# x transposed unscaled and kept for the residual, and part of the output projection between attention steps

## The chip, the core and the metric

The kernel runs on one core of a Trainium2 chip. The metric is the device time of one execution in microseconds (us). A core has five engines that run side by side and meet at semaphores: TensorE (matrix products and transposes, into eight banks of accumulators), VectorE, ScalarE (ACT), GpSimd (POOL) and SyncE (SP), which here issues nearly all loads and stores to 16 DMA engines.

## What is computed

One layer of a hybrid encoder over 320 rows: 256 prompt frames and 64 sample frames, 1024 features, all in 32-bit floats. Cut to what matters here:

```python
h = rms_norm(x, p['norm_mix'])            # x * rsqrt(mean(x^2) + eps) * gain
proj = h @ p['w_in']                      # u, z, a, b, cq, ckv, kpe
...                                       # o_gdn: 4 recurrent (gated delta) heads
...                                       # o_mla: 4 latent-attention heads
mix = jnp.concatenate([o_gdn.reshape(B, S, GDN_VW), o_mla.reshape(B, S, MLA_HEADS * V_DIM)], axis=-1)
x = x + mix @ p['w_out']
h = rms_norm(x, p['norm_mem'])            # then attention over 256 memory tokens
x = x + om.reshape(B, S, MEM_HEADS * MEM_HEAD_DIM) @ p['w_mo']
h = rms_norm(x, p['norm_ffn'])            # then a router and 32 experts, top 4
x = x + y.reshape(B, S, D)
```

Each expert has three weight matrices of 1024 x 1024, so 12.6 MB, and all 32 are run.

## The kernel before

The kernel is written engine by engine, in one order per engine; `CHAIN` lists the steps of the first part in the order in which every engine takes its share of them. Nothing is scheduled by a tool: the order of the code is the order of each queue, and semaphores (`wait_ge`, `then_inc`) join the queues. `mark` and `at` set and read one-time events of an engine.

**Layouts.** Rows are kept in three blocks of 128, 128 and 64 (`TB` = 3, `b`); features in eight blocks of 128 (`KD` = 8, `k`). `x3` is x by rows. `hT` is feature-major: `hT[:, k, :]` is feature block k on the partitions and 320 columns. A product of a 128 x 128 weight block with `hT[:, k, :]` is one `mm` of 320 columns; in the trace it is two MATMUL instructions, since the operands are 32-bit. A transpose (`tr`) is one.

**Start.** SP loads x, the constants (`CO`: identity, ones, masks, the epsilon column) and then the blocks of `w_in`. ACT issues ten small loads (the convolution's rows and eight gain vectors) and squares the three row blocks (`squares`). VectorE and POOL turn the sums into reciprocal norms (`rstd`, `root`), VectorE scales the rows into `xs3`. TensorE transposes the convolution's rows and the gains, then the scaled rows in `norm_transposes`, 24 transposes over banks 0 and 1 in turn; ACT copies each bank into `hT` with the gain `c_mix` (`feature_major`). Then `project(pos, ...)` works through `RING`: each position is a tile of 128 outputs, eight products over k, banks 0 and 1 in turn, moved out by ACT in `evacuate`.

**Middle.** Recurrent heads and latent attention are prepared in `CHAIN`. The recurrent heads' results (`o_gdn`) stand in `hT[:, 0:4, :]` before the attention starts; the attention heads' results go to `hT[:, 4:8, :]` one by one. `attention("mla", ...)` has 12 units (3 row blocks x 4 heads) and 15 steps n; in a step TensorE does the scores of unit n, transposes the probabilities of unit n-2 and multiplies those of unit n-3 with the values. Between the steps `conv_states_and_x(n)` is called on TensorE and ACT: from n = `XT_AT` = 7 on it transposes one feature block k of x, which SP has loaded a second time into `x3`, over banks 6 and 7, and ACT copies it to `xT[:, k, :]` and scales a block of the memory queries' weights (`wmq_sb`) with the gain.

**Output projection.** For each k, eight products of `wout_sb` with `hT` (i = 0 to 3 the recurrent heads, 4 to 7 the attention heads) in bank k % 2; `x2_add(k)` on VectorE adds them to `xT[:, k, :]`, and four products of the memory queries follow for the block before. Then comes the memory attention (`attention("mem", ...)`), the router, and the experts.

**Experts.** Weights stream through nine slots of 2 MB (`slot_sb`, `tile_at`; six tiles an expert). Slots 0 to 5 are the tile `weights`, 6 lies in `stream`, 7 in `small_weights`, 8 is `more_weights` (`W2`), which nothing else uses. `first_tiles` fills a slot for the first time, as the space comes free; `refill` waits for `tile_used`, that is for TensorE to have gone through the tile nine places before.

## Time and profile before

| | us |
|---|---|
| Median of 3 runs | 1323.24 (1319.42 to 1323.3) |
| The profiled execution | 1321.59, span 1319.8 |
| TensorE busy in the span | 1275.2 (97%) |
| VectorE, ACT, GpSimd busy | 462.7, 215.1, 19.5 |
| Loaded and stored | 440.53 MB, mean 334 GB/s |

The profile is one execution. Its page lists busy time and the chain of work that ended last: followed back from the last instruction, at each step to what released it. Four stretches can be told apart: the first part up to the attention (to 248 us), the attention with its last steps (to 283), the output projection and memory attention (to 384), and, after the router, the experts from 401 on. TensorE's granted clock is 1.00 (2.4 GHz) or 0.50 (1.2 GHz). A busy TensorE is not one at its peak: ends of matmuls are modelled, and a few records can be missing.

### The profile page before, as it was taken

To read this page: it belongs to the slowest core of one execution; us is meant where nothing else is said; L and a number is where in the kernel's file an instruction comes from. 1 tells how busy PE (TensorE), PEld (TensorE's weight loads), DVE (VectorE), ACT (ScalarE), POOL (GpSimd) and SP (SyncE) were. 2 spreads that over 40 slices of the span, in tenths; PEclk is the share of its full clock that TensorE was granted. 3 is DMA by queue.
4 is the path that set the end of the run, shared out by engine and by line. 5 is a ranking of instruction groups with operands and counts; after the bars stand their busy time and mean duration, and the time that the engine had idled before them with its cause. 6 is when DMAs were issued, how large, how long until landed. Compare 5 with 4: busy or idle time off the path is not lost.

```text
span 1319.8 us, 21031 instructions
## 1 busy us (share of the span) xinstructions
PE 1275.2 (97%) x8602; PEld 580.3 (44%) x8602; DVE 462.7 (35%) x984; ACT 215.1 (16%) x573; POOL 19.5 (1%) x28
## 2 busy tenths in 40 slices
PE   5999999999999999999999999999999999999997
PEld 4677655567564333433333433333433333333332
DVE  2455234533664233322333322333322333322223
ACT  3551333740341000000000000000000000000000
POOL 0000011100000000000000000000000000000000
PEclk9999999989989999999999999999999999999999
DMA  9512100852238999999999999999999999999996
GB/s 337 216 65 89 42 29 16 296 200 110 80 124 344 428 428 427 429 429 429 429 428 429 429 428 428 428 428 429 429 429 429 429 429 429 429 428 429 429 428 261
DMA packets 48046, 440.53 MB, mean 334 GB/s; under 512 B 7635, under 2 KB 10169, under 8 KB 23334
## 3 DMA queue, kind: packets, MB, share of 16 engines
q1 hardware_dynamic: 47916, 439.90, 80.1%
q8 instruction: 29, 0.48, 0.1%
q14 instruction: 11, 0.09, 0.0%
q10 hardware_dynamic: 90, 0.06, 0.0%
HBM read 436.62 MB, written 3.33 MB: 333 GB/s over the span
## 4 chain that ended last, share of the span: by engine, by line
PE 78%; DMA 16%; DVE 3%; ACT 2%; issue 1%; POOL 1%; DVEq 0%; SPq 0%; POOLq 0%
PE bank L1053 74%; DMA weights<-in_w_gu 15%; PE bank L1056 3%; ACT scaled L614 1%; POOL stats L586 1%; DMA x<-in_x_sample 1%; ACT stream L614 0%; PE bank L1692 0%; DVE weights L1818 0%; DVE x L2391 0%; ACT weights L614 0%; DVE x L2240 0%; DVE stats L2161 0%; ACT small_weights L614 0%; DVE scaled L1822 0%
## 5 line engine op out<-in xcount | busy, mean ns | idle before, releaser
L2391 DVE SCALAR_TENSOR_TENSOR x<-bank,small_weights,x 128x512 f32<-128x512 f32 (+1 forms) x192 | 134.9, 744 | 598.5 <-PE bank L1053 598.5
L1053 PE MATMUL bank<-weights,small_weights 128*64 128x512 f32 (+4 forms) x1456 | 336.0, 588 | 3.1 <-DMA weights<-in_w_gu 3.1
L1053 PEld LDWEIGHTS bank<-weights,small_weights 128*64 128x64 f32 (+1 forms) x1456 | 105.7, 139 | 195.6 <-issue 171.6
L1053 PE MATMUL bank<-weights,scaled 128*64 128x512 f32 x704 | 155.9, 595 | 5.1 <-ACT scaled L614 5.1
L614 ACT ACTIVATE scaled<-bank 128x256 f32<-128x256 f32 (+5 forms) x153 | 58.2, 408 | 324.9 <-PE bank L1053 241.9
L614 ACT ACTIVATE scaled<-scaled 128x512 f32<-128x512 f32 x32 | 20.2, 631 | 550.0 <-DVE scaled L1822 550.0
L1053 PE MATMUL bank<-scaled,small_weights 64*128 64x512 f32 x384 | 108.1, 640 | 1.4 <-DVE x L2391 0.7
L1053 PE MATMUL bank<-stream,small_weights 128*64 128x512 f32 (+4 forms) x408 | 89.5, 547 | 2.1 <-DMA stream<-in_w_gu 1.1
L1053 PEld LDWEIGHTS bank<-weights,scaled 128*64 128x64 f32 x704 | 48.7, 137 | 97.1 <-issue 87.9
L1053 PE MATMUL bank<-small_weights 96*64 96x512 bf16 (+2 forms) x408 | 86.7, 497 | 0.5 <-DVE small_weights L1818 0.5
L1053 PEld LDWEIGHTS bank<-stream 128*128 128x128 bf16 (+1 forms) x2416 | 75.0, 100 | 27.5 <-issue 26.4
L1053 PE MATMUL bank<-small_weights,weights 128*128 128x320 f32 (+3 forms) x320 | 86.2, 419 | 0.6 <-ACT small_weights L614 0.6
L1053 PE MATMUL bank<-stream 128*128 128x64 bf16 (+1 forms) x2416 | 79.2, 196 | 1.1 <-ACT stream L614 1.1
L1053 PEld LDWEIGHTS bank<-small_weights,weights 128*128 128x128 f32 (+2 forms) x320 | 57.0, 190 | 24.8 <-issue 3.7
L1053 PE MATMUL bank<-weights 64*64 64x64 f32 (+5 forms) x752 | 65.7, 266 | 0.0
L1053 PEld LDWEIGHTS bank<-scaled,small_weights 64*128 64x128 f32 x384 | 29.0, 184 | 79.0 <-issue 75.9
L1053 PEld LDWEIGHTS bank<-small_weights 96*64 96x64 bf16 (+2 forms) x408 | 28.7, 128 | 70.0 <-issue 67.9
L1053 PE MATMUL bank<-small_weights,stream 128*128 128x320 f32 (+4 forms) x212 | 57.0, 427 | 0.0
L1053 PEld LDWEIGHTS bank<-stream,small_weights 128*64 128x64 f32 (+1 forms) x408 | 31.6, 146 | 51.3 <-issue 44.4
L1053 PEld LDWEIGHTS bank<-weights 64*64 64x64 f32 (+3 forms) x752 | 38.7, 144 | 22.4 <-issue 21.0
L1053 PEld LDWEIGHTS bank<-small_weights,stream 128*128 128x128 f32 (+1 forms) x212 | 37.4, 195 | 16.8 <-issue 3.5
L1053 PE MATMUL bank<-more_weights,small_weights 128*64 128x512 f32 x176 | 40.2, 598 | 0.5 <-DMA more_weights<-in_w_gu 0.5
(194 smaller groups left out, 903.1 us busy)
## 6 DMA issues: line engine op xcount, KB each, us to landing
weights<-in_w_gu SPq DMA_DIRECT2D x85, 2048.0 KB, 26.9
weights<-in_w_down SPq DMA_DIRECT2D x44, 2048.0 KB, 28.3
stream<-in_w_gu SPq DMA_DIRECT2D x21, 2048.0 KB, 28.1
more_weights<-in_w_gu SPq DMA_DIRECT2D x11, 2048.0 KB, 27.7
small_weights<-in_w_gu SPq DMA_DIRECT2D x11, 2048.0 KB, 26.2
small_weights<-in_w_down SPq DMA_DIRECT2D x10, 2048.0 KB, 28.2
more_weights<-in_w_down SPq DMA_DIRECT2D x10, 2048.0 KB, 28.4
weights<-in_w_in SPq DMA_DIRECT2D x4, 2048.0 KB, 14.4
```

Source lines behind the costliest of these rows:

```text
L586: pool.tensor_tensor(tile, tile, minus_half[0:tile.shape[0], :].broadcast_to(list(tile.shape)), ALU.pow).then_inc(sem("root_ready"), 1)
L614: return act.activation(out, in_, func, **kw)
L1053: return pe.matmul(out, lhsT, rhs, start=start, stop=stop)
L1056: return pe.transpose(out, in_, ident[0:in_.shape[0], 0:in_.shape[0]])
L2391: dve.scalar_tensor_tensor(xx, PS[bank][0:rows, :], gcur[0:rows, b:b + 1], xx, ALU.mult, ALU.add)\
```

## The change

Five things change.

1. **Start.** x is loaded as three blocks with semaphores of their own. The first 260 columns of the constants, put in another order, come by ACT's queue, ahead of the small loads; the rest by SP behind the first block of `w_in`, which is split in two. TensorE transposes the unscaled x3, block by block as it arrives, into all eight banks; ACT copies each bank to `xraw`, which lies in `W2`. ACT squares two row blocks and VectorE the third; ACT takes the reciprocal root with a logarithm and an exponential. VectorE writes the reciprocals on diagonals, TensorE multiplies these with ones, so that every partition has the row of 320 reciprocals, VectorE copies it to `rstd_rows`, and one operation per k makes `hT` from `xraw`, gain and `rstd_rows`. The first projection's product k waits for that `hT` block alone.
2. **No second load of x,** and no transposes of it between attention steps: `x2_add` reads `xraw`.
3. **Output projection.** Between the last attention steps TensorE does the products i = 0 to 3 of k = 0 and k = 1, into banks 6 and 7. After the attention only i = 4 to 7 remain for these two.
4. **Slot 8** is loaded for the first time behind the last `x2_add`, since `xraw` lies in it.
5. The loads of `w_out`'s two halves have semaphores of their own, and the loads of `b_gu` no longer wait for the transposes of x.

The diff, cut to its core:

```diff
-            load(x3[:, 0:2, :], b_major(x_prompt[0]), "ld_x")
-            load(x3[0:DEC, 2, :], x_sample[0], "ld_x")
-            load(CO[:, :], consts, "ld_const")
-            load(wqk_sb[:, :, 512:1024], k_major(w_in[0][:, 512:1024], 0, KD), "ld_win0")
+            for b in range(2):
+                load(x3[:, b, :], x_prompt[0][b * P:(b + 1) * P, :], f"ld_x{b}")
+            load(x3[0:DEC, 2, :], x_sample[0], "ld_x2")
+            for n in range(2):
+                load(wqk_sb[:, 4 * n:4 * n + 4, 512:1024], k_major(w_in[0][:, 512:1024], 4 * n, 4 * n + 4), f"ld_win0{'ab'[n]}")
+            load(CO[:, C_HEAD:C_N], consts[:, C_HEAD:C_N], "ld_const")
...
-            first_tiles(SLOTN - 1, SLOTN)
...
-            load(x3[:, 0:2, :], b_major(x_prompt[0]), "ld_x")
-            load(x3[0:DEC, 2, :], x_sample[0], "ld_x")
...
-            sp.wait_ge(sem("xT_tr"), KD)
...
+            sp.wait_ge(sem("x2_add"), KD)
+            first_tiles(SLOTN - 1, SLOTN)
             sp.wait_ge(*at("qm_mm"))
             first_tiles(0, 1)
...
+            act.dma_start(CO[:, 0:C_HEAD], consts[:, 0:C_HEAD]).then_inc(sem("ld_head"), 16)
...
+            for b in range(2):
+                act.wait_ge(sem(f"ld_x{b}"), 16)
+                run(x_junk[b], x3[:, b, :], ACT.Square, accum_out=ssq[:, b:b + 1]).then_inc(mark(f"x{b}_sq"), 1)
+            act.wait_ge(sem("ld_head"), 16)
+            act.wait_ge(*at("x1_sq"))
+            act.wait_ge(*at("x2_sq"))
+            run(ssq[:, 0:3], ssq[:, 0:3], ACT.Ln, scale=1.0 / D, bias=eps_col).then_inc(mark("x_logs"), 1)
+            act.wait_ge(*at("x_logs"))
+            run(ssq[:, 0:3], ssq[:, 0:3], ACT.Exp, scale=-0.5).then_inc(mark("x_rstd"), 1)
             for k in range(KD):
-                feature_major(k, (0, 1), "x", hT, None, c_mix, T)
+                act.wait_ge(sem("rows_tr"), k + 1)
...
+                run(xraw[:, k, :], PS[k][:, 0:T]).then_inc(sem("xraw_ev"), 1)
...
+            pe.wait_ge(sem("ld_head"), 16)
+            for b in range(TB):
+                rows = P if b < 2 else DEC
+                pe.wait_ge(sem(f"ld_x{b}"), 16)
+                for k in range(KD):
+                    m = tr(PS[k][:, b * P:b * P + rows], x3[0:rows, b, k * P:(k + 1) * P])
...
+            pe.wait_ge(*at("diag0"))
+            mm(PS[5][:, 320:448], ones, rstd_diag[:, 0, :])
+            pe.wait_ge(*at("diag2"))
+            mm(PS[5][:, 448:512], ones[0:DEC, :], rstd_diag[0:DEC, 2, 0:DEC]).then_inc(mark("rbc02_mm"), 1)
+            pe.wait_ge(*at("diag1"))
+            mm(PS[7][:, 320:448], ones, rstd_diag[:, 1, :]).then_inc(mark("rbc1_mm"), 1)
...
                 for k in range(k0, k1):
+                    if pos == 0:
+                        pe.wait_ge(sem("rows_ev"), k + 1)
...
+                for g in {GO_AT: (0, 1)}.get(n, (n - GO_AT + 1,) if n > GO_AT else ()):
+                    k, i = g // 4, g % 4
+                    if i == 0:
                         pe.wait_ge(sem("cs_ev"), 5 + k)
+                        pe.wait_ge(sem("ld_wgo"), 16)
+                    mm(PS[6 + k][:, 0:T], wout_sb[:, i, k * P:(k + 1) * P], hT[:, i, :], i == 0, False)
...
-                    for i in range(KD):
+                    for i in range(4 if k < 2 else 0, KD):
...
+            dve.wait_ge(sem("ld_x2"), 16)
+            link(tt(x_junk[2][0:DEC, :], x3[0:DEC, 2, :], x3[0:DEC, 2, :], ALU.mult))
+            dve.tensor_reduce(ssq[0:DEC, 2:3], x_junk[2][0:DEC, :], AX, ALU.add).then_inc(mark("x2_sq"), 1)
...
+            for b in (0, 2, 1):
+                ts(rstd_diag[:, b, :], ident, ssq[:, b:b + 1]).then_inc(mark(f"diag{b}"), 1)
...
+            for k in range(KD):
+                dve.wait_ge(sem("xraw_ev"), k + 1)
+                dve.scalar_tensor_tensor(hT[:, k, :], xraw[:, k, :], c_mix[:, k:k + 1], rstd_rows, ALU.mult, ALU.mult)\
+                    .then_inc(sem("rows_ev"), 1)
...
-                tt(xT[:, k, :], xT[:, k, :], PS[k % 2][:, 0:T], ALU.add).then_inc(sem("x2_add"), 1)
+                tt(xT[:, k, :], xraw[:, k, :], (PS[6 + k] if k < 2 else PS[k % 2])[:, 0:T], ALU.add).then_inc(sem("x2_add"), 1)
```

How the instructions stand on an engine, in the program before and in the changed one. In these lists a product of two operands is `out<-moving,weights` by the names of the tiles, with its size; the waits are the semaphores.

TensorE up to the first projection, before. `scaled` is the scaled x, `small_weights` is `hT`:

```order
L1056 MATMUL bank7<-const,stream 128x7 [waits ld_rows,ld_const]
L1056 MATMUL bank7<-const,stream 128x7 x11
L1056 MATMUL bank6<-const,stream 128x38
L1056 MATMUL bank0<-const,scaled 128x128 [waits row_scaled]
L1056 MATMUL bank0<-const,scaled 128x128 x2
L1056 MATMUL bank1<-const,scaled 128x128 x3
L1056 MATMUL bank0<-const,scaled 128x128 [waits rows_ev]
...
L1053 MATMUL bank0<-small_weights,weights 128x320 [waits ld_win0,rows_ev]
L1053 MATMUL bank0<-small_weights,weights 128x320 x7
```

The same place in the changed program. `x` is the unscaled x, `more_weights` here the diagonals:

```order
L1065 MATMUL bank0<-const,x 128x128 [waits ld_x0,ld_head]
...
L1065 MATMUL bank0<-const,x 128x128 [waits ld_x1]
...
L1065 MATMUL bank0<-const,x 128x64 [waits ld_x2]
...
L1065 MATMUL bank4<-const,stream 128x38 [waits ld_rows]
L1062 MATMUL bank5<-more_weights,const 128x128 [waits vector_events]
L1062 MATMUL bank5<-more_weights,const 128x64 [waits vector_events]
L1062 MATMUL bank7<-more_weights,const 128x128 [waits vector_events]
L1065 MATMUL bank6<-const,stream 128x7 [waits ld_conv]
L1065 MATMUL bank6<-const,stream 128x7 x11
L1062 MATMUL bank0<-small_weights,weights 128x320 [waits ld_win0a,rows_ev,xraw_ev]
L1062 MATMUL bank0<-small_weights,weights 128x320 [waits rows_ev] x3
```

The 24 transposes of x moved from behind the scaling to the front, three small products came between, and the convolution's transposes moved from the first place to the last ahead of the projections.

TensorE in the last attention steps (n = 13 and 14) and at the head of the output projection, before:

```order
L1053 MATMUL bank5<-small_weights,weights 128x64 [waits att_o,att_pt]
L1053 MATMUL bank5<-small_weights,weights 128x64 x2
...
L1053 MATMUL bank4<-small_weights,weights 128x64 x2
L1056 MATMUL bank7<-const,x 128x128 [waits xT_ev]
L1056 MATMUL bank7<-const,x 128x128
L1056 MATMUL bank7<-const,x 128x64
L1053 MATMUL bank5<-small_weights,weights 128x64 [waits att_o,att_pt]
L1053 MATMUL bank5<-small_weights,weights 128x64 x2
L1053 MATMUL bank0<-small_weights,stream 128x320 [waits ld_wout,xT_ev]
L1053 MATMUL bank0<-small_weights,stream 128x320 x3
L1053 MATMUL bank0<-small_weights,stream 128x320 [waits att_o]
L1053 MATMUL bank0<-small_weights,stream 128x320 x3
```

and in the changed program:

```order
L1062 MATMUL bank7<-small_weights,stream 128x320
L1065 MATMUL bank3<-const,small_weights 128x64 [waits att_pt,att_nm]
...
L1062 MATMUL bank4<-small_weights,weights 128x64 x2
L1062 MATMUL bank7<-small_weights,stream 128x320
L1062 MATMUL bank5<-small_weights,weights 128x64 [waits att_o,att_pt]
L1062 MATMUL bank5<-small_weights,weights 128x64 x2
L1062 MATMUL bank6<-small_weights,stream 128x320 [waits att_o,ld_wout,wmq_ev]
L1062 MATMUL bank6<-small_weights,stream 128x320 x3
L1062 MATMUL bank7<-small_weights,stream 128x320 x4
```

Three transposes of x gave place to one product of the output projection, and the first product behind the attention now waits for the last head (`att_o`).

SP's queue from the loads for the output projection to the first expert tiles, before:

```order
L420 DMA x<-in_x_prompt 128x2x1024 [waits kT_ev,qT_ev,st_state]
L420 DMA x<-in_x_sample 64x1024
L420 DMA weights<-in_w_mq 128x8x512
...
L420 DMA x<-in_b_gu 32x2048 [waits xT_tr]
...
L420 DMA stream<-in_w_router 128x8x32 [waits x2_mm]
L420 DMA stream<-in_b_down 32x1024 x3
L420 DMA weights<-in_w_gu 128x4096 [waits tensor_events]
L420 DMA weights<-in_w_gu 128x4096 [waits x3_mm]
```

and in the changed program:

```order
L423 DMA weights<-in_w_mq 128x8x512 [waits kT_ev,qT_ev,st_state]
...
L423 DMA x<-in_b_gu 32x2048 x3
...
L423 DMA stream<-in_w_router 128x8x32 [waits x2_mm]
L423 DMA stream<-in_b_down 32x1024 x3
L423 DMA more_weights<-in_w_gu 128x4096 [waits x2_add]
L423 DMA weights<-in_w_gu 128x4096 [waits tensor_events]
L423 DMA weights<-in_w_gu 128x4096 [waits x3_mm]
```

The second load of x is gone, `b_gu` waits for nothing of its own, and slot 8 stands behind the small loads of the router.

## Rows read from the trace of the kernel before

**Rows 1.** The page: its span, the chain by line, TensorE's clock in 40 slices

```profile
span 1319.8 us, 21031 instructions
...
PEclk9999999989989999999999999999999999999999
...
PE bank L1053 74%; DMA weights<-in_w_gu 15%; PE bank L1056 3%; ACT scaled L614 1%; POOL stats L586 1%; DMA x<-in_x_sample 1%; ACT stream L614 0%; PE bank L1692 0%; DVE weights L1818 0%; DVE x L2391 0%; ACT weights L614 0%; DVE x L2240 0%; DVE stats L2161 0%; ACT small_weights L614 0%; DVE scaled L1822 0%
```

**Rows 2.** Instructions in order of time, first 26 us (start, us, engine, tiles, releaser)

```profile
7.87 1.06 ACT L614 ACTIVATE weights<-x 128x1024 f32<-128x1024 f32 x1 [1.90 <-DMA x<-in_x_sample]
...
10.22 1.67 PE L1056 MATMUL bank<-const,stream 7*128 7x7 f32 x13 [10.22 <-DMA stream<-in_mq_norm]
...
14.77 1.14 PEld L1056 LDWEIGHTS bank<-const,scaled 128*128 128x128 f32 x6 [3.03 <-DVE scaled L1822]
...
19.39 0.32 PEld L1056 LDWEIGHTS bank<-const,scaled 128*128 128x128 f32 x3 [0.38 <-ACT small_weights L614]
...
21.20 5.11 PE L1053 MATMUL bank<-small_weights,weights 128*128 128x320 f32 x18 [0.62 <-ACT small_weights L614]
...
25.81 0.38 ACT L614 ACTIVATE stream<-bank 128x256 f32<-128x256 f32 x1 [4.66 <-PE bank L1053]
```

**Rows 3.** Instructions in order of time: prices of operations on VectorE and ACT

```profile
11.93 0.20 ACT L614 ACTIVATE gain_cols<-bank 128x38 f32<-128x38 f32 x1
...
26.91 1.74 DVE L1915 SCALAR_TENSOR_TENSOR stream<-stream,stats 128x323 f32<-128x323 f32 x3
...
222.87 0.69 DVE L1841 TENSOR_REDUCE stats<-weights 128x4 f32<-128x512 f32 x1
...
228.92 0.95 DVE L1818 TENSOR_TENSOR x<-x,stats 64x768 f32<-64x768 f32 x1 [1.11 <-POOL stats L586]
```

**Rows 4.** Instructions in order of time, last attention steps and output projection

```profile
265.22 0.58 PE L1056 MATMUL bank<-const,x 128*128 128x128 f32 x3
265.73 1.43 PE L1053 MATMUL bank<-weights 128*64 128x320 f32 x4
...
283.11 0.22 DVE L2173 COPY small_weights<-bank 128x64 f32<-128x64 f32 x1 [2.35 <-PE bank L1053]
```

**Rows 5.** Stretches: length, busy (count) of PE, PEld, DVE, ACT, POOL; clock, DMA share, GB/s

```profile
21.20:25.50 4.30, 4.30 (x16) 3.11 (x17) 0.00 (x0) 0.00 (x0) 0.00 (x0) 1.00 1.08 342
276.00:278.70 2.70, 2.70 (x21) 2.04 (x20) 1.18 (x5) 2.16 (x11) 0.00 (x0) 1.00 0.00 0
278.70:282.00 3.30, 3.30 (x15) 2.56 (x13) 0.23 (x1) 1.91 (x7) 0.00 (x0) 0.51 0.00 0
285.00:289.00 4.00, 4.00 (x8) 2.46 (x8) 0.00 (x0) 0.00 (x0) 0.00 (x0) 0.50 1.01 371
291.00:331.00 40.00, 40.00 (x150) 28.21 (x149) 13.98 (x18) 3.31 (x7) 0.00 (x0) 1.00 0.37 156
...
343.60:347.00 3.40, 1.94 (x13) 1.41 (x14) 3.26 (x12) 1.15 (x5) 0.00 (x0) 1.00 0.29 125
```

**Rows 6.** SP's queue in order of time; then one stretch, columns as in rows 5

```profile
123.44 0.58 SPq L420 DMA_DIRECT2D more_weights<-in_w_gu  x1
...
405.86 0.35 SPq L540 DMA_DIRECT2D weights<-in_w_gu  x1
...
346.00:384.00 38.00, 37.13 (x180) 21.83 (x182) 21.46 (x68) 15.77 (x43) 1.63 (x4) 1.00 0.00 1
```

**Rows 7.** The chain that ended last, in order of time (start, us, what)

```profile
448.80 27.28 PE bank L1053 x186
...
1123.57 40.16 DMA weights<-in_w_gu
...
1167.64 40.13 DMA weights<-in_w_gu
```

More of the change, by code:

```diff
@@ L494, in _ @@
             sp.wait_ge(sem("cl_tr"), 7)
-            for n in range(2):
-                load(wout_sb[:, 4 * n:4 * n + 4, :], k_major(w_out[0], 4 * n, 4 * n + 4), "ld_wout")
+            load(wout_sb[:, 0:4, :], k_major(w_out[0], 0, 4), "ld_wgo")
+            load(wout_sb[:, 4:8, :], k_major(w_out[0], 4, 8), "ld_wout")
             sp.wait_ge(sem("mk_ev"), 4)
@@ L1138, in project @@
                 for k in range(k0, k1):
+                    if pos == 0:
+                        pe.wait_ge(sem("rows_ev"), k + 1)
+                        if k == 0:
+                            pe.wait_ge(sem("ld_win0a"), 16)
+                        elif k == 4:
+                            pe.wait_ge(sem("ld_win0b"), 16)
                     if kind == "clp":
@@ L2401, in _ @@
             gates()
-            dve.wait_ge(sem("ld_ffn"), 16)
             rows_in(0)
```

148 lines of the change are left out of this document (72 added, 76 removed).

## Prediction

> **What bounds the kernel now.** I read the page first. The span is 1319.8 us, and the chain of work that ended last is almost all TensorE, with 15% in the loads of expert weights [rows 1]. So only what moves the start of TensorE's work, or the stream of expert tiles, can move the end. Then the chain in order of time: an expert is one block of 27.28 us of products, and late in the run the chain passes through the tile loads instead, 40.13 us in one piece [rows 7]. Early experts are paced by TensorE, late ones by the queue. That queue refills a slot only when TensorE releases it, and its first refill is issued at 405.86 [rows 6], 4 us after TensorE began expert 0. From there both run without a gap. A gain ahead of that release therefore moves the whole stream and arrives at the end in full. Last, the two places that the diff touches: the start up to the first projection [rows 2], and the last attention steps with the output projection behind them [rows 4, 5].
>
> **The start.** Now: the squares begin at 7.87, when the last x row is in; TensorE does the weights' small transposes at 10.22; the scaled rows are transposed from 14.77; the first projection begins at 21.20 and is moved out of its bank from 25.81. A projection is 16 instructions in 4.3 us [rows 5], so the second can begin at 25.5.
>
> The change removes the scaling of x on VectorE and GpSimd's power; TensorE transposes raw x between 5 and 9 us, beside the loads. Nothing waits for that. What ends last is the reciprocal norm, step by step:
> - x is in at about 8.2 (7.87, plus up to a tenth for the 0.13 MB of constants that now travel with it).
> - The 64 sample rows are squared on VectorE. 768 elements take 0.95 and a reduction of 512 takes 0.69 [rows 3]; at their slope of 0.26 per 256 elements 1024 take 1.2 each: 10.7.
> - Two small ACT steps at 0.20 [rows 3] with hand-offs: 11.2. Three diagonals of 128 columns, 0.3 and then 0.2 each, three products of them with ones, three copies of 0.3: the last copy at 13.1. No row has these shapes, so the six steps might take 1.5 or 2.5; I take 1.9.
> - The first of eight fused scalings (three of 323 elements take 1.74, so 0.58 each [rows 3]): 13.7.
> - On TensorE the 12 transposes of the convolution's rows stand ahead of the projections. 13 such took 1.67 [rows 2], and they can start at 12.6: 14.2. That is the first product.
>
> At which rate do the products then run? The granted clock is at nine tenths or more from the first slice of the page's strip [rows 1], but the rows say otherwise: six weight loads took 1.14 at 14.77 and three took 0.32 at 19.39, 0.19 against 0.11 each [rows 2]. In the stretch with a granted clock of 0.50, eight records fall in 4 us, where 150 fall in 40 at full rate [rows 5]. So the engine began at half rate here, and reached the full one only after some 4.5 us of transposes. The Trainium skill (TensorE: Matmul & The Clock Gate, What's actually happening) says the same, that an idle array is throttled and activity releases it, and it speaks against this change, because the work that used to warm the engine is now followed by a pause. If one took the strip at its word, the projection would end at 18.5 and the gain would be 7.0.
>
> I take the rows: about 5 us at half rate (1.07 a product, 4.7 of them), then 3.3 at 0.54: end at 21.0, a gain of 4.5 on 25.5. The bounds are 2.7 (half rate throughout, end 22.8) and 7.0 (full rate at once).
> VectorE's 0.58 per scaling hides behind 1.07, and costs at most 0.3 in all at full rate. ACT's eight copies of the raw tiles run ahead of the scalings. The weights: the first projection's 2 MB now stand ahead of most of the constants, and later projections come some 4 us sooner than now, while their loads were issued back to back; I find no wait of TensorE for one in this stretch now, so 0.
>
> **The last attention steps.** Removed: 24 transposes of reloaded x in eight groups of three, and eight ACT copies. A group takes 0.51 (265.22 to 265.73) [rows 4]: 4.1 us at full rate. Added in their place: eight products of 320 columns, two instructions of 0.267 each [rows 5], 4.3 us, plus 0.1 for a weight load that nothing covers, for seven of them: 5.0. VectorE and ACT wait for TensorE here, so their shorter lists give nothing. Cost 0.9 (0 to 1.2).
> Removed from the output projection: the same eight products, 4.3 us. Added there: the first product now needs the last head. Four products hid that hand-over; now TensorE waits for a copy of 0.22 and its two hand-offs, as the row at 283.11 shows the copy [rows 4]: 0.4. Together: 4.3 - 0.9 - 0.4 = 3.0 (bounds 2.3 to 3.9).
>
> **The clock at this place.** The granted clock fell at 278.7 and was back at 289.0 [rows 5]; 10.3 us at half rate cost 5.1. Before it fell, TensorE did groups of 64-column products, small transposes and the three x transposes, with no idle time in the record. In the memory attention at 343.6 to 347, whose products have 256 columns, it stayed at 1.00, though TensorE had idle time there [rows 5]. The change puts a 320-column product into each of these thin steps. I think it more likely than not that the clock then holds: 5.1 us more.
>
> **The loads.** x is not loaded a second time (1.25 MB, queued ahead of the query weights; those come sooner, which nobody waited for). The ninth expert tile moves from 123.44 [rows 6] to behind the x2 additions, near 330. After it the DMA engines are idle from 346 to 384 [rows 6]; a tile takes 4.9 us (nine slots turn over in the 44.07 between the load pieces at 1123.57 and 1167.64 [rows 7]). So it is hidden; if that cover were gone, 4.9. b_gu and the tiles behind it no longer wait for the transposes and start some 15 us earlier, on idle engines: 0.
>
> **The sum.** 4.5 + 3.0 + 5.1 = 12.6. The profiled execution took 1321.59 (span 1319.8 plus 1.8) and becomes 1309.0; it lies 1.65 under the median of 1323.24, which becomes **1310.6**.
>
> **Rivals.**
> - *The clock falls again.* For it: TensorE was never idle in 276 to 278.7, and still it fell [rows 5]; the thin steps are still thin. Same sum without the 5.1: 1315.7. The Trainium skill (same page, HAM oscillation — how this bites in real kernels) blames gaps between matmuls; the measurement decides here, since the fall came with no such gap.
> - *The gain is absorbed by the tile stream.* 15% of the chain is loads [rows 1]. If the stream were bound by its own start, the end would not move: 1323. Against it: its first issue follows TensorE's release [rows 6], and 346 to 384 is idle.
> - *Slower: the clock stays low in the projections.* Their start is now stop-and-go: transposes, waits for diagonals, then products. Each product at half rate costs 0.53 more, a projection 4.3. With the first one wholly at half rate the sum is 2.7 + 3.0 + 5.1 = 10.8. Each further one takes 4.3 from it, so from three and a half more the time is 4 us above the old one; for six more it is 25.8 - 10.8 = 15.0 above, 1338. Against it: in the old start, transposes alone raised the clock within 5 us [rows 2].
> - *The late row loads.* The ten small loads ended the wait at 10.22 [rows 2]; the convolution's are now last. Each us past 12.6 costs one: with 4 us more, 1314.6, inside the range.
>
> **How the numbers follow.** Forecast 0.56; clock falls again 0.30; small loads or another hold-up at the start 0.06 (still faster); absorbed 0.05; slower 0.03. Likeliest: 1310.6. Its own range with the start's bounds and some 1.5 of noise is 1306.6 to 1314, the first rival's 1313 to 1318. Together 1306 to 1317.5, with some 0.15 outside. About 0.3%, 4 us, is what a measurement can tell from no change: faster 0.91, same 0.06, slower 0.03.
>
> **What would show it.** In the changed profile: raw transposes between 5 and 9 us; the first projection's product near 14 and its copy near 21.3 (above 23 the start's term is wrong, below 19.5 the engine was warm); weight loads of 0.19 beside the first products; in the last attention steps groups of two 320-column instructions; the granted clock at 1.00 through them and into the output projection (if it shows 0.50 for 10 us, the rival holds); eight products fewer after the last head; tile nine landed by 345; the first refill near 393.3; 27.28 us an expert as before. It would be wrong by another mechanism if TensorE waited for weights in the first 40 us, or if the first refill came earlier and the end did not.

## The result

The changed kernel takes 1312.59 us, median of 4 runs (1310.99 to 1313.69), beside 1322.01 of the kernel before on the same chip (4 runs, 1319.42 to 1323.3): ratio 0.9935, 95% interval 0.9922 to 0.9948. A second series (f0_after, below) gave 0.9928 (0.9915 to 0.9941). The forecast was 1310.6, 12.6 us off the kernel before; the medians differ by 9.4, the spans of the two profiled executions by 10.6 (1319.8 and 1309.2). By the gain the median is nearer to the first rival (7.5, the sum without the clock's 5.1) than to the forecast, and the profiles are nearer to the forecast.

The page after: the span, the chain by line, and TensorE's clock in 40 slices, which answer to [rows 1].

```profile
span 1309.2 us, 21006 instructions
...
PEclk9999999999979999999999999999999999999999
...
PE bank L1062 75%; DMA weights<-in_w_gu 15%; PE bank L1065 2%; ACT scaled L617 1%; DMA x<-in_x_sample 0%; POOL stats L590 0%; ACT stream L617 0%; PE bank L1713 0%; DVE weights L1839 0%; DVE x L2426 0%; DVE x L2275 0%; DVE stats L2196 0%; DVE scaled L1839 0%; DVE x L1839 0%; DVE weights L1950 0%
```

The dip that stood in the ninth slice before is gone; the one in the twelfth is deeper, 7 where it was 8. The start after, in order of time, beside [rows 2]:

```profile
5.02 3.27 PEld L1065 LDWEIGHTS bank<-const,x 128*128 128x128 f32 x16 [5.02 <-DMA const<-in_consts]
...
9.04 1.21 DVE L1903 TENSOR_REDUCE stats<-scaled 64x1 f32<-64x1024 f32 x1
...
11.36 2.14 PE L1062 MATMUL bank<-more_weights,const 128*128 128x128 f32 x6 [1.17 <-DVE more_weights L1843]
...
13.43 1.44 PE L1065 MATMUL bank<-const,stream 7*128 7x7 f32 x12
13.54 0.29 DVE L1912 COPY more_weights<-bank 128x128 f32<-128x128 f32 x1 [0.30 <-PE bank L1062]
...
14.80 15.49 PE L1062 MATMUL bank<-small_weights,weights 128*128 128x320 f32 x51
...
20.91 0.50 ACT L617 ACTIVATE stream<-bank 128x256 f32<-128x256 f32 x2 [5.04 <-PE bank L1062]
```

The diagonals' products and the convolution's transposes stand between the squares and the first projection, whose bank is moved out at 20.91 instead of 25.81. The last attention steps, and then SP's queue, beside [rows 4] and [rows 6]:

```profile
275.89 0.81 PE L1062 MATMUL bank<-small_weights,stream 128*128 128x320 f32 x2
276.53 0.92 PE L1062 MATMUL bank<-small_weights,weights 128*128 128x64 f32 x6
277.86 4.54 PE L1062 MATMUL bank<-small_weights,stream 128*128 128x320 f32 x16 [0.41 <-DVE small_weights L2208]
```

```profile
323.16 0.42 SPq L423 DMA_DIRECT2D more_weights<-in_w_gu  x1
...
395.43 0.35 SPq L544 DMA_DIRECT2D weights<-in_w_gu  x1
```

Last the stretches (length, busy and count of PE, PEld, DVE, ACT, POOL; granted clock, DMA share, GB/s), beside [rows 5]:

```profile
14.80:17.80 3.00, 3.00 (x7) 2.02 (x7) 2.95 (x8) 0.90 (x3) 0.00 (x0) 1.00 1.04 385
18.00:20.90 2.90, 2.90 (x12) 2.09 (x11) 0.41 (x1) 0.00 (x0) 0.00 (x0) 1.00 1.06 403
...
270.60:277.40 6.80, 6.80 (x40) 4.92 (x39) 2.19 (x9) 4.91 (x15) 0.00 (x0) 1.00 0.56 234
...
376.30:384.20 7.90, 5.86 (x38) 5.37 (x38) 6.26 (x25) 4.41 (x10) 0.73 (x2) 0.50 1.01 431
384.25:388.30 4.05, 4.05 (x75) 4.05 (x75) 3.55 (x16) 1.16 (x1) 0.00 (x0) 0.50 1.02 431
389.00:393.20 4.20, 4.17 (x12) 1.34 (x14) 4.09 (x6) 0.00 (x0) 0.00 (x0) 0.50 0.02 8
393.40:397.60 4.20, 4.20 (x24) 1.34 (x22) 2.17 (x5) 0.00 (x0) 0.00 (x0) 1.00 0.37 74
```

**Where the time went.** The same steps in both traces give the gain as it stands at each place: 4.8 at the end of the start (75.38 became 70.55 for one block of products); 12.4 behind the output projection (342.70 became 330.26, for the same VectorE operation); 12.5 at the first expert's first product (401.55 became 389.03); 10.4 at the first refill (405.86 became 395.43); 10.6 at the end. So the two edited places brought what was forecast for them together, and 2.1 were lost inside the first expert tile. The last two of these rows show how: TensorE did 12 instructions in the first 4.2 us of expert 0 and 24 in the next 4.2. Before, it had done the same place at full rate:

```profile
401.60:405.80 4.20, 4.20 (x22) 1.52 (x24) 4.06 (x7) 0.00 (x0) 0.00 (x0) 1.00 0.01 6
```

The clock had been low ahead of the experts in both, from 388.0 to 401.6 before and from 376.3 to 393.3 after; it came back as the experts began before (401.55), and 4.3 us into them after. All this is one execution of each kernel; the runs as a whole, in the section on the clock in all runs, say less for the clock.

### The profile page after: what moved, and what is told of

Its sections match the earlier page's. It is cut to its first block, busy times and chain, and to the rows that moved or that the text cites. A ratio compares the mean times of both kernels' runs of the same rounds, so it can differ in the third digit from the quotient of the medians.

```text
span 1309.2 us, 21006 instructions
## 1 busy us (share of the span) xinstructions
PE 1271.8 (97%) x8584; PEld 577.3 (44%) x8584; DVE 467.2 (36%) x996; ACT 209.8 (16%) x565; POOL 18.6 (1%) x27
## 4 chain that ended last, share of the span: by engine, by line
PE 78%; DMA 16%; DVE 3%; ACT 2%; issue 1%; POOL 0%; SPq 0%; DVEq 0%; ACTq 0%; POOLq 0%
PE bank L1062 75%; DMA weights<-in_w_gu 15%; PE bank L1065 2%; ACT scaled L617 1%; DMA x<-in_x_sample 0%; POOL stats L590 0%; ACT stream L617 0%; PE bank L1713 0%; DVE weights L1839 0%; DVE x L2426 0%; DVE x L2275 0%; DVE stats L2196 0%; DVE scaled L1839 0%; DVE x L1839 0%; DVE weights L1950 0%
## 5 line engine op out<-in xcount | busy, mean ns | idle before, releaser
L617 ACT ACTIVATE scaled<-bank 128x512 f32<-128x512 f32 (+6 forms) x145 | 54.8, 406 | 322.9 <-PE bank L1062 241.8
```

The costliest lines, as they stand in the source:

```text
L617: return act.activation(out, in_, func, **kw)
```

## The experiments

Each ran 4 to 12 times, beside 9 to 17 runs of the kernel before on its chip. Ratios are to that kernel. "Theory" and "rival" are those of the text printed ahead of each result. The profile is one of the runs, not the median one.

**One part undone.** e1_no_early: the changed kernel with all products of the output projection behind the attention.

```diff
-                for g in {GO_AT: (0, 1)}.get(n, (n - GO_AT + 1,) if n > GO_AT else ()):
...
-                    for i in range(4 if k < 2 else 0, KD):
+                    for i in range(KD):
```

> The changed kernel with its eight early products of the output projection put back behind the attention; x is still not reloaded, so the last attention steps now have neither x transposes nor 320-column products in them. Against the changed kernel (1312.6): the attention gets shorter by the eight products (5.0) and by the wait for the last head (0.4), the output projection longer by 4.3, so -1.1 before the clock is counted. Theory (a 320-column product in each thin step is what held the clock): TensorE's granted clock falls to 0.50 somewhere in 270 to 290 for some 10 us, as in the kernel before, which costs 5: 1316.5. Rival (it was the transposes of x, now gone, that let it fall): the clock stays at 1.00 there and the kernel is faster than the changed one, 1311.5.

The median is 1313.93, ratio 0.9940 (0.9918 to 0.9961), single runs from 1309.65 to 1317.37. The profile has two low stretches here, and TensorE was busy all through them:

```profile
252.50:259.10 6.60, 6.60 (x21) 3.49 (x18) 2.43 (x11) 2.62 (x9) 0.00 (x0) 0.50 0.94 346
259.30:276.20 16.90, 16.81 (x93) 10.07 (x93) 10.34 (x42) 12.33 (x41) 0.00 (x0) 1.00 0.67 236
276.40:283.00 6.60, 6.60 (x16) 4.40 (x16) 1.14 (x2) 1.26 (x1) 0.00 (x0) 0.50 1.01 380
```

The clock fell at the end of the attention, as the theory has it, but the median lies between the two expectations. By the ratios the kernel is 0.7 to 1.6 us above the changed one, where the theory wanted 3.9 and the rival 1.1 below it, and its interval reaches about as far as both. Whether this order is the cheaper one by products alone the times do not show: its best run (1309.65) is faster than any of the changed kernel's first series, but not than the best of its second (1308.63).

**One part alone.** e2_start_only: as e1_no_early, and x is reloaded and transposed between the steps, as before.

```diff
+            load(x3[:, 0:2, :], b_major(x_prompt[0]), "ld_xr")
+            load(x3[0:DEC, 2, :], x_sample[0], "ld_xr")
...
+                        m = tr(PS[6 + k % 2][:, b * P:b * P + rows], x3[0:rows, b, k * P:(k + 1) * P])
```

> Only the start of the change: x is loaded a second time and transposed between the attention steps, and all 64 products of the output projection stand behind the attention, as in the kernel before; the ninth slot's first load stays where the change put it. Theory (the parts of the gain add up): the start's 4.8 us alone come off the kernel before, 1317.2, with the clock low for some 10 us at the end of the attention as before. The changed kernel stands 5 to 7 us below that. Rival (the start's gain is given back before the experts, by a longer stretch at half rate there, whenever the program is shifted): 1319 to 1320, with a stretch at 0.50 of 17 us ahead of the first expert tile. If the attention part should be worth nothing, this kernel is as fast as the changed one, 1312.6.

The median is 1318.19, ratio 0.9973 (0.9961 to 0.9985): 2 to 5 us gained by the interval, 3.6 in the middle, where 4.8 were expected. Its profile is low from 273.8 to 284.1 and from 383.1 to 396.7, and its span of 1314.6 is 5.2 under the one before. The start's part is real and by itself some 4 us. The rest of the change adds 5 to 6 more (0.9973 against 0.9935 and 0.9928). Of that, e1_no_early, on the same chip, has 4.3 by the medians (1318.19 and 1313.93), and what separates it from this kernel is the second load of x with its transposes and copies. So most of what the change gains behind the start comes from the transposes that went, for which the prediction had 4.1.

**The loss ahead of the experts.** e3_keep_gate: products whose results nobody reads, in TensorE's pauses.

```diff
+            def dummy(bank, *widths):
+                for w in widths:
+                    mm(PS[bank][:, 0:w], ones, CO[:, C_US:C_US + w])
...
+            dummy(3, 512, 256)
             rows_feature_major(2)
+            dummy(3, 512)
             router(2)
...
+            dummy(5, 512, 512)
             pe.wait_ge(sem("x3_part"), 2 * TB)
             gather(0, ((0, 1), (2,)))
+            dummy(2, 256)
```

> The changed kernel with seven added products whose results nobody reads (512 or 256 columns, constants by constants, into banks that are free), in the pauses of TensorE between the router and the first expert: 512 and 256 columns behind router(1), 512 behind the last block's transposes, 512 ahead of the last ranks, twice 512 ahead of the gather, 256 behind it. The profile after has 0.50 from 376.3 to 393.3. Theory (the thin work of the router lets the clock fall, and this is where 2.1 us of the forecast gain went): with the pauses filled the clock stays at 1.00, the gather's 4.0 us become 2.0 to 2.5, the first expert tile is used in 4.3 instead of 6.4, its refill is issued near 391, and the end moves by as much: 1308.5. Rival (these steps are paced by VectorE and the clock costs nothing, or falls anyhow): the added products only stand in the way, 1313 to 1314.5.

The median is 1307.68, ratio 0.9902 (0.9885 to 0.9920), as the theory has it. One of the six runs took 1312.0, at the same granted clock of 0.996 as the others, which nothing here explains. The same steps as in the stretches above:

```profile
376.30:384.00 7.70, 7.23 (x48) 4.61 (x47) 7.16 (x29) 4.56 (x11) 0.73 (x2) 1.00 1.01 434
384.07:386.30 2.23, 2.23 (x76) 2.23 (x75) 2.06 (x7) 1.20 (x1) 0.00 (x0) 1.00 1.02 430
388.05:392.30 4.25, 4.25 (x22) 1.54 (x24) 4.11 (x7) 0.00 (x0) 0.00 (x0) 1.00 0.31 131
```

The gather (which collects the rows of the first expert) takes 2.2 instead of 4.05, the first tile is used in 4.3 instead of 6.4, and its refill goes out at 392.34. The end lies 914 us behind it, as it did behind the refill in the profiles before and after.

**The start.** e4_warm_start: ten such products, four of 512 columns ahead of the transposes of x, one of 192 ahead of its second block, one ahead of its third, and four ahead of the diagonals' products. The expectation counts nine.

```diff
+            dve.memset(hT[:, 0:3, :], 0.5).then_inc(mark("warm_ready"), 1)
...
+            for n in range(4):
+                warm(6 + n % 2, 0, 512)
...
+                if b:
+                    warm(6, 320, 192)
...
+            for n in range(4):
+                warm(6, 320, 192)
```

> The changed kernel with nine added products whose results nobody reads, on a tile that VectorE fills first: four of 512 columns before x is in, one of 192 between the blocks of x, four of 192 ahead of the diagonals' products. In the profile after, the clock rose at 17.9, 3.1 us into the first projection, and the three diagonals' products took 2.14. Theory (TensorE begins at half rate because it has done too little): the clock is up before the first product, that comes at 14.0 instead of 14.8, the first projection is out at 18.5 to 19 instead of 20.9, and the kernel gains 2: 1310.5. Rival (it begins at half rate whatever it does, or falls again in the pauses): no gain, the added products delay the transposes, 1312.6 to 1314.

The median is 1308.62, ratio 0.9897 (0.9881 to 0.9914), better than the theory's 1310.5. TensorE's rows:

```profile
1.89 6.63 PE L1062 MATMUL bank<-small_weights 128*128 128x512 f32 x8 [1.89 <-DVE small_weights L1907]
...
12.93 1.16 PE L1062 MATMUL bank<-more_weights,const 128*128 128x128 f32 x6
14.03 0.90 PE L1065 MATMUL bank<-const,stream 7*128 7x7 f32 x12
15.12 1.31 PE L1062 MATMUL bank<-small_weights,weights 128*128 128x320 f32 x4 [0.18 <-ACT more_weights L617]
```

The four wide products' eight instructions took 6.63 and held the transposes up until 8.35, so the first product of the projection came 0.3 later than in the changed kernel, not 0.8 earlier. But four of its instructions took 1.31, and the first copy stands at 19.70 instead of 20.91. This trace gains 1.2 there. By the ratios the kernel gains 4.1 to 5.0, more than the trace shows. The granted clock of its runs is 0.992 to 0.994, that of the changed kernel's 0.987 to 0.993, so it was low for less time; where, and why an edit of the start should do that, is not shown.

**The changed kernel again.** f0_after, unaltered.

> The changed kernel once more, unaltered, for a second profile and for runs beside the next three. Theory (where TensorE's work is thin, whether and for how long the granted clock falls differs from one execution to the next): the time stays at 0.9935 of the kernel before, 1312.5, with single runs spread over 3 us, and the profile shows other low stretches than 376.3 to 393.3, perhaps one near 250 as in e4_warm_start. Rival (the low stretches belong to the program): the same one stretch of 17 us ahead of the experts.

The median is 1311.43, ratio 0.9928 (0.9915 to 0.9941), with runs from 1308.63 to 1314.19. Theory and rival were both half right: ahead of the experts its stretch is again 376.4 to 393.4, while the start differs. The clock was up from 7.7, fell at 11.1 and came back at 18.0:

```profile
7.80:11.10 3.30, 1.36 (x14) 0.94 (x12) 2.43 (x2) 1.35 (x5) 0.00 (x0) 1.00 1.05 373
11.20:17.90 6.70, 6.41 (x24) 4.83 (x25) 5.23 (x15) 2.90 (x10) 0.00 (x0) 0.50 1.04 393
```

**All thin places at once.** f1_all_kept, cut to two of its edits (an added product in a pause near 248 us, and the last early product moved behind the attention):

```diff
+                if n == 3:
+                    dummy(4, 512)
...
+                            mm(PS[7][:, 0:T], wout_sb[:, 3, P:2 * P], hT[:, 3, :], False, False)
```

> The changed kernel with products whose results nobody reads at all thin places at once: the seven of e3_keep_gate; a leaner start than e4_warm_start's (three of 512 columns ahead of x, one of 192 ahead of the third block, two ahead of the diagonals); and one of 512 columns in the 1.1 us pause near 248, where two profiles had the clock fall. And the last of the eight early products stands behind the attention, where TensorE waited 0.41 for the last head. Theory: the clock rises before 11 and holds at 1.00 to the end; first projection out near 18 instead of 20.9 (3), 4 to 4.7 before the first refill, 0.4 for the wait: 1304.5, and its runs spread less than those of the changed kernel. Rival (the parts share their gain, since a fall that is prevented here comes later elsewhere): 1307.5, no better than e3_keep_gate.

The median is 1308.45, ratio 0.9908 (0.9895 to 0.9921): no better than e3_keep_gate, so the sum failed. The clock was up at 5.5, fell in the start from 12.3 to 19.1, and from 381.0 to 384.4, among the unread products ahead of the gather; the gather itself, from 385.17, took 2.26, as at full rate. So the parts were not all achieved. g1_richest below speaks for their adding up where they are.

f2_kept_no_early is f1_all_kept with e1_no_early's edit.

> f1_all_kept with all eight early products behind the attention, as in e1_no_early. Counted in products alone this is cheaper: 5.0 less in the attention, 4.3 more behind it, and no wait for the last head in either: f1_all_kept less 0.7. Theory (the early products pay only by holding the clock in the thin steps from 268 to 278): the clock falls there in most executions, for 7 to 10 us, and the kernel is 2 to 4 us slower than f1_all_kept. Rival (it holds there as well once x is no longer transposed in these steps): 0.7 faster than f1_all_kept, and the early products were never worth anything.

The median is 1309.71, ratio 0.9910 (0.9898 to 0.9923): 1.3 slower by the medians, less than the theory's 2 to 4, and the two ratios cannot be told apart. The profile shows the fall that the theory named, at half rate from 271.6:

```profile
271.70:278.40 6.70, 6.70 (x19) 4.89 (x19) 1.36 (x3) 2.28 (x6) 0.00 (x0) 0.50 0.89 320
```

**The first refill.** f3_split: its first half is loaded when half of tile 0 has been used.

```diff
+                if n == SLOTN:
+                    sp.wait_ge(*at("half_used"))
+                    sp.dma_start(dst[:, 0:2 * FF], src[:, 0:2 * FF]).then_inc(sem("ld_half"), 16)
+                    sp.wait_ge(sem("tile_used"), 1)
+                    sp.dma_start(dst[:, 2 * FF:4 * FF], src[:, 2 * FF:4 * FF]).then_inc(sem(name), 16)
```

> f1_all_kept with the first refill cut in two: its first MB is loaded once TensorE has used the first half of tile 0, its second MB once it has used the whole; nothing else of the stream changes. In every profile so far the end of the span lies 913.2 to 914.1 us behind the issue of the first refill. Theory (that issue sets the end, since the queue is idle for some 4 us before it and full from there): the first MB goes out 2.1 us earlier and the end comes 2 us earlier than f1_all_kept's. Rival (TensorE's own pace sets the end by then, or the halves lose at the queue what they win): within 0.5 us of f1_all_kept.

The median is 1308.30, ratio 0.9905 (0.9891 to 0.9919), as f1_all_kept. Here the start held its clock, and the first expert began at 385.95, 2.3 sooner than in f1_all_kept; the halves went out early, but the span is only 0.4 shorter:

```profile
388.33 0.33 SPq L551 DMA_DIRECT2D weights<-in_w_gu  x1
390.05 0.33 SPq L553 DMA_DIRECT2D weights<-in_w_gu  x1
```

The stretch from 408 to 416, of f1_all_kept and then of f3_split:

```profile
408.00:416.00 8.00, 8.00 (x42) 2.80 (x40) 0.00 (x0) 0.60 (x1) 0.00 (x0) 1.00 1.01 430
```

```profile
408.00:416.00 8.00, 8.00 (x42) 2.69 (x40) 0.00 (x0) 0.60 (x1) 0.00 (x0) 1.00 0.96 358
```

The queue moved 358 GB/s there instead of 430: it had run ahead and waited for TensorE's later releases. So the first issue does not set the end. Something else took back most of what expert 0 had won, too: the end lies 919.7 us behind its first product here, and 917.8 in f1_all_kept (919.2 in g4_richest_split below, 918.4 in e3_keep_gate). Either the cut itself costs that 1 to 2 us, or the stream of tiles holds the end back when the experts begin this early; no profile without the cut has them this early.

**Fuller.** g1_richest has more unread products in the start, and the early products of the output projection in thinner steps:

```diff
-                for g in {GO_AT: (0, 1)}.get(n, (n - GO_AT + 1,) if n > GO_AT else ()):
+                for g in {8: (0,), 9: (1,), 10: (2,), 11: (3,), 12: (4, 5), 13: (6,)}.get(n, ()):
```

> f1_all_kept with a fuller start and the early products moved into the thinner steps. Start: three unread products of 512 columns, one of 192 ahead of the second and the third block of x, four of 192 ahead of the diagonals, and one of 256 (constants) behind the convolution's transposes; in f1_all_kept the clock rose at 5.5 and fell again from 12.3 to 19.1, in f3_split, with the same start, it held. Early products: one each in steps 8 to 11 and 13, two in step 12, the last behind the attention. Theory (f1_all_kept came out at 1308.5 and not at 1304.5 because its clock still fell in the start and in the gather): the clock holds throughout, the experts begin near 386 and the time is 1305.5 to 1306.5. Rival (with the experts begun by 388 the tile queue sets the end, and what is won ahead of them no longer counts): the experts begin at 386 and the time stays at 1307.5 to 1308.5; the end then lies more than 915 us behind the first refill.

The median is 1305.39, ratio 0.9883 (0.9868 to 0.9898), with runs from 1304.14 to 1308.61: **the lowest median of this study**, 6 to 7 us below the changed kernel by the ratios. Its interval overlaps those of e3_keep_gate and e4_warm_start. The profiled execution is its longest (span 1306.7): the clock held in its start and its router, but fell from 274.3 to 281.1, and the experts began at 388.66. The other three runs have no profile, but a granted clock of 0.998 to 0.999 over the span, against 0.997 in this one, and spans of 1302.3 to 1304.2; so the clock held nearly throughout, as the theory has it. And the rival, that the tile queue sets the end once the experts begin by 388, is out as far as these spans reach. g4_richest_split adds f3_split's cut.

> g1_richest with the first refill cut in two as in f3_split. In f3_split the first MB went out 4.2 us earlier than the refill of f1_all_kept, but the end of the span moved only 0.4, and the queue had a pause at 408 to 416 that it had not had. Theory (once refills start as early as this they soon wait for TensorE's next release, so that what is won at the front of the queue is lost 20 us later): within 0.5 us of g1_richest. Rival (f3_split only differed by its clock, and the cut is worth its 2 us): 2 us faster than g1_richest.

The median is 1306.12, ratio 0.9894 (0.9878 to 0.9909): the cut is worth nothing, or costs a little. Its profile is the one in which the clock never fell between the start and the last microseconds:

```profile
5.80:100.00 94.20, 92.18 (x628) 65.16 (x627) 49.88 (x129) 43.61 (x111) 0.71 (x1) 1.00 0.57 203
100.00:1300.00 1200.00, 1177.89 (x7989) 508.23 (x7988) 415.68 (x861) 165.61 (x456) 17.69 (x22) 1.00 0.83 348
```

Its experts begin at 385.09, 3.9 us before those of the changed kernel, and its span is 1304.3, the shortest of all profiles (two runs of g1_richest, at 1302.3 and 1302.9, were shorter).

**The wait for the last head.** g2_gate_behind: e3_keep_gate with one early product moved behind the attention.

> e3_keep_gate with the last of the eight early products put behind the attention, ahead of the wait for the last head; the start is the changed kernel's own. Theory (in the changed profile TensorE waits 0.41 there, and that wait stands on the path): e3_keep_gate less 0.4, 1307.3; in the profile no wait ahead of the first product behind the attention. Rival (one product fewer in step 14 lets the clock fall there): 1309 or more.

The median is 1308.55, ratio 0.9912 (0.9899 to 0.9926), by the ratios 1.3 above e3_keep_gate and not 0.4 below it. The wait is gone in the profile (products at 279.84 follow those begun at 277.92 without a pause), but the clock fell from 279.7 to 283.2, as the rival has it, and also from 252.4 to 255.8. A gain of 0.4 us can't be told from that: the experiment is inconclusive.

**The ninth slot.** g3_slot8_late: its first load behind slot 7's.

```diff
             sp.wait_ge(sem("x2_add"), KD)
-            first_tiles(SLOTN - 1, SLOTN)
...
-            first_tiles(TILES + 1, SLOTN - 1)
+            first_tiles(TILES + 1, SLOTN)
```

> The changed kernel with the first load of the ninth slot moved further back, from behind the x2 additions (issued at 323.2 in the profile after) to behind the load of slot 7 (379.9), so that nothing idle covers it ahead of the experts. Theory (it was hidden by the queue's idle time; four tiles then stand in a row, and the queue is idle from about 390.5 to 396 only): most of its 4.9 us falls into that pause, the refills' own loads begin 0 to 0.5 us later, time as the changed kernel or up to 0.5 above, 1312 to 1312.5. Rival (every tile loaded later moves the end by its 4.9): 1316.5.

The median is 1313.53, ratio 0.9948 (0.9934 to 0.9961): 1.7 to 2.6 us above the changed kernel's two series by the ratios, with overlapping intervals. The theory wanted at most 0.5, the rival 3.9. The rows:

```profile
380.16 0.33 SPq L423 DMA_DIRECT2D small_weights<-in_w_gu  x1
380.53 0.43 SPq L423 DMA_DIRECT2D more_weights<-in_w_gu  x1
393.95 0.35 SPq L543 DMA_DIRECT2D weights<-in_w_gu  x1
```

The tile landed at 395.8, in what had been idle time; the end lies 914 behind the refill here too. In this profile, then, the tile was hidden. But it is the fastest of the five runs (1309.74); the other four took 1312.69 to 1313.94 at a granted clock of 0.992 and 0.993, where the changed kernel's three runs at these values took 1308.63 to 1312.04. So some 2 us or more of the tile's 4.9 may show in most executions; how much is left open.

**The clock in all profiles.** When it was first up, and each stretch at 0.50 after that (the last microseconds left out; the runs by the first two characters of their names):

| Profile | first up | low in the start | low at 250 to 290 | low ahead of the experts |
|---|---|---|---|---|
| before | 19.4 | | 278.8-289.0 | 388.0-401.6 |
| e2 | 17.8 | | 273.8-284.1 | 383.1-396.7 |
| e1 | 20.3 | | 252.4-259.2, 276.3-283.1 | 382.1-395.7 |
| after | 17.9 | | | 376.3-393.3 |
| f0 | 7.7 | 11.1-18.0 | | 376.4-393.4 |
| g3 | 18.0 | | | 376.4-390.1 |
| e4 | 7.8 | | 250.2-257.0 | 379.9-390.1 |
| e3 | 8.3 | 11.8-18.6 | | |
| g2 | 20.3 | | 252.4-255.8, 279.7-283.2 | |
| f1 | 5.5 | 12.3-19.1 | | 381.0-384.4 |
| f2 | 5.4 | 12.2-19.0 | 271.6-278.5 | |
| f3 | 7.7 | | 273.9-277.3 | |
| g1 | 8.0 | | 274.3-281.1 | |
| g4 | 5.8 | | | |

At the end of the attention the clock fell in 4 of 4 profiles without the early products, and in 3 of 10 with them. Of these ten, none of the five with all eight products between the steps fell there, and three of the five that have the last one behind the attention (g2, f1, f3, g1, g4). Ahead of the experts it fell in 7 of 7 without the added products, and in 1 of 7 with them.

**The clock in all runs.** Each run on record, with or without a profile, has its granted clock over the span. A thousandth less is 2.6 us more at 0.50; the time ahead of the first rise counts as full speed, so a start that rises early and falls again reads lower than one that rises late. The mean was 0.990 in the kernel before (37 runs, 0.988 to 0.993) and 0.990 in the changed kernel too (10 runs, 0.987 to 0.993). It was 0.988 in e2, 0.989 in e1, 0.993 in e4 and g3, 0.994 in f2, 0.995 in f1, 0.996 in e3 and g2, 0.997 in f3, and 0.998 or more in g1 and g4. Two things follow. The profiled execution of the changed kernel (0.993) is one of the two best of its ten, and over all runs the change did not raise the clock. And the clock goes with most of the spread between runs: the changed kernel's two runs at 0.993 took 1308.63 and 1310.99, its three at 0.987 took 1313.69 to 1314.19.

## Why the prediction held, point by point

**The bound.** Right. In the profiles before and after, and in g3_slot8_late, the end lies 913.8 to 913.9 us behind the first refill, and in the others without a cut refill 913.2 to 914.1. Experts take 27.28 us of products each, and the tile loads 40.16, as in [rows 7]:

```profile
410.15 27.28 PE bank L1062 x186
...
1113.17 40.16 DMA weights<-in_w_gu
```

What f3_split and g4_richest_split add: this distance is a marker, not the cause. With the first refill issued earlier by a cut, it was 917.3 and 916.8, and the time was no better.

**The start.** The total was right, 4.9 against 4.5 (e2_start_only, over 12 runs, has 3.6), by two errors that partly cancel. The step of the reciprocals was too cheap: ACT's steps ended at 10.90, and from there diagonals, products and copies took 2.9 instead of 1.9, the diagonals' six instructions 2.14 of them (1.16 in e4_warm_start, where the clock was up). So the last copy ended at 13.8, not 13.1, and the first product came at 14.8, not 14.2. And the half rate was too long: 3.1 us of the projection (7 instructions in 3.0, then 12 in 2.9), not 5. The granted clock reads 1.00 in both of these rows; the prediction trusted the durations, and that was the right choice.

**The last attention steps.** The forecast was a cost of 0.9 and a wait of 0.4; the wait is 0.41 in the row above. From the same transposes, at 260.36 and at 255.53, to the first product behind the attention, the trace before has 22.64 us, some 2.1 of them due to the half rate from 278.8 on, and the trace after has 22.33. That is 1.8 more at full rate, 0.4 of it the wait, so the eight products cost 0.5 more than forecast. Beside narrow products one takes 0.73 (271.88 to 272.61), not 0.63. Behind them 4.3 fewer, as forecast.

**The clock at this place.** It held in the changed kernel's profile and in f0_after's, so the forecast case came out there, and between the two profiles this term was worth 5. Over all runs it was worth far less, and that is where most of the difference between 12.6 and 9.4 lies. Putting the early products in gained 0.7 to 1.6 by the ratios (e1_no_early to the changed kernel), where the expectation has 3.9 for it, and 1.3 by the medians in f2_kept_no_early to f1_all_kept; both differences lie within the noise. With the 1.1 that the products cost by the sum, the clock gave back some 2 to 3 us, an estimate, and not 5.1. The parts by experiment are 3.6 for the start, 4.3 for the transposes that went and 0.7 to 1.6 for the early products, in all the 8.6 to 9.5 of the ratios. That the median fell into the range with a clock term of about half the size is partly luck. f3_split, g1_richest and g2_gate_behind, which have seven early products between the steps and one behind the attention, lost the clock at this place; whether the eighth makes the difference is open, with 0 of 5 profiles against 3 of 5. The rule of the Trainium skill that the prediction weighed (TensorE: Matmul & The Clock Gate, HAM oscillation — how this bites in real kernels) seeks the cause in gaps between matmuls. The fall of e1_no_early at 276.3 came behind a stretch with TensorE busy 16.81 of 16.90 us (the row above), that of f2_kept_no_early at 271.6 behind 8.50 of 8.60, so for this place the measurement speaks against it again. The fall of e1_no_early at 252.4 is another matter: it came behind a pause, 3.29 busy of 4.40 us.

**The term that was missing.** The prediction put the refill at 393.3 and it came at 395.43. It looked at the clock at the start and at the end of the attention, and not between the router and the experts, where the kernel before was already low for 13.7 us. There the sum took the old trace over unchanged. e3_keep_gate shows what stood there: 1307.68 with the clock held. By the ratios, that is 3.4 to 4.4 us below the changed kernel. Of these the profile shows 2.1 inside the first tile and 1.0 ahead of it (expert 0 at 388.05 instead of 389.03); the rest is not placed. The kernel before loses time at this place too, so what the change itself lost here is only the 2.1 between the two profiles. Whether the longer stretch (17.1 against 13.7) belongs to the changed kernel or to the execution is open: two of its profiles have 17.1, and g3_slot8_late, whose TensorE work is the same, has 13.7.

**The loads.** The ninth tile landed at 331.6, before 345. No product waited for weights in the first 40 us. Whether this much cover is needed g3_slot8_late leaves open.

**The rivals.** Absorption is out (10.4 of 12.5 arrive at the end). So are late row loads (the gains were transposed at 9.87 and the convolution at 13.43, behind the diagonals) and a clock that stays low through several projections (the latest rise in any profile is 20.3).

## What to carry to other kernels

Before an edit is priced, list every stretch in which TensorE's clock is low, and also every one in which its work is thin, from the rate of the instructions and not from the strip alone; each is a term of the sum that can come or go whether or not it was edited. Where such a stretch stands on the path, a few products into a free bank, whose results nobody reads, can be worth microseconds if they fit the pause (3.4 to 4.4 here, for seven of them). A change that costs 1 us by instructions and is to gain 5 by the clock is to be judged by many executions, and by their granted clock, not by one profile: here two profiles show the clock's 5 in full, and the medians some 2 to 3 of it.

## What was not expected of the hardware

- The same program met different clocks in different executions. The start that the changed kernel, e1, e2, e3, f0, g2 and g3 share had its clock first up at 17.9, 20.3, 17.8, 8.3, 7.7, 20.3 and 18.0, and in two of these it fell again. The Trainium skill (TensorE: Matmul & The Clock Gate, What's actually happening) says that the rise varies from run to run, by half a microsecond either way. The rows agree that it varies, but by 12.6 us between the earliest and the latest, and show it for the falls as well.
- Half rate cost small instructions less than a factor of two: twelve small transposes took 1.44 ahead of the clock's first rise (changed kernel) and 0.90 behind it (e4_warm_start), a factor of 1.6; the gather took 4.05 and 2.23, a factor of 1.8.
- Runs of one kernel spread over 1.4 to 8 us (f2_kept_no_early and e1_no_early, the latter from 1309.65 to 1317.37), as much as most edits here are worth.
